# Two chained transformer blocks on one core: products, norms and transposes at a stage's edge taken by groups of 128 tokens, without unread products, with eight slots for split weights

## The reference, cut to what matters

```python
for layer in range(2):                       # first block
    x = x + mixers(rmsnorm(x, norm_mix[layer]) @ w_in[layer])
    x = x + memory_cross_attention(rmsnorm(x, norm_xattn[layer]), ...)
    gate, up = jnp.split(rmsnorm(x, norm_ffn[layer]) @ w_gate_up[layer], 2, axis=-1)
    x = x + (jax.nn.silu(gate) * up) @ w_down[layer]
x = rmsnorm(x, norm_final)
for layer in range(2):                       # second block
    h = swiglu(rms_norm(x, g[0]), ffn_w_in[layer, 0], ffn_w_out[layer, 0])
    x = x + 0.5 * rms_norm(h, g[1])
    h = hybrid_mixer(rms_norm(x, g[2]), ...) if layer == 0 else recurrent_mixer(rms_norm(x, g[2]), ...)
    x = x + rms_norm(h, g[3])
    h = swiglu(rms_norm(x, g[4]), ffn_w_in[layer, 1], ffn_w_out[layer, 1])
    x = x + 0.5 * rms_norm(h, g[5])
```

## Time and profile before

| what | value |
|---|---|
| median of 3 runs | 2314.92 us (2310.24 to 2315.61) |
| the profiled execution's own time | 2307.78 us |
| its span | 2306.3 us |
| mean granted TensorE clock | 0.981 |
| PE busy | 2164.6 us, 94% |
| DVE, ACT busy | 1389.6 us (60%), 1122.4 us (49%) |

### The profile page before, as it was taken

One profiled execution on the slowest core, in us unless ns is written; L12 is line 12 of the kernel. 1 busy time (PEld: TensorE's weight loads), 2 busy tenths in 40 slices (PEclk: granted clock), 3 DMA queues, 4 the chain that ended last, 5 costly groups with the idle time before them and its releaser, 6 DMA issues.

```text
span 2306.3 us, 25337 instructions
## 1 busy us (share of the span) xinstructions
PE 2164.6 (94%) x10018; PEld 1758.5 (76%) x10018; DVE 1389.6 (60%) x1929; ACT 1122.4 (49%) x1741; POOL 33.2 (1%) x45
## 2 busy tenths in 40 slices
PE   8998798999999888999999999979999999979998
PEld 6866677888886667788778877657788788767886
DVE  5966665554695765555455547564655555566553
ACT  5545355444544535544354446534544444475442
POOL 0000000000000000000000000100000000000000
PEclk9999999999999999999999999989999999989999
DMA  6652243555554225355545545303455455534553
GB/s 225 202 198 73 92 165 116 190 189 186 182 183 164 76 89 176 116 184 186 196 157 184 196 169 173 126 37 129 172 185 192 178 184 183 192 127 137 183 185 125
DMA packets 52805, 369.27 MB, mean 160 GB/s; under 512 B 6191, under 2 KB 6447, under 8 KB 9040
## 3 DMA queue, kind: packets, MB, share of 16 engines
q1 hardware_dynamic: 48960, 356.54, 43.4%
q10 hardware_dynamic: 3216, 9.53, 1.3%
q0 software_dynamic: 512, 1.57, 0.3%
HBM read 366.31 MB, written 1.31 MB: 159 GB/s over the span
## 4 chain that ended last, share of the span: by engine, by line
PE 85%; DVE 8%; ACT 5%; issue 1%; DMA 0%; POOL 0%; ACTq 0%; DVEq 0%
PE ps L447 25%; PE ps L449 25%; PE ps L448 25%; PE ps L493 2%; PE ps L549 2%; DVE ring_lo L1023 1%; ACT upper_w L1697 1%; PE ps L658 1%; PE ps L477 1%; DVE x L1173 1%; ACT z L1754 1%; DVE S L1094 1%; DVE xn L1161 1%; PE ps L732 0%; DVE PTs L1108 0%
## 5 line engine op out<-in xcount | busy, mean ns | idle before, releaser
L1023 DVE TENSOR_TENSOR ring_lo<-ring,upper_w 128x1024 fp32r<-128x1024 f32 x659 | 803.4, 1227 | 535.5 <-ACT upper_w L1697 529.9
L1697 ACT CAST upper_w<-ring 128x1024 fp32r<-128x1024 f32 x659 | 689.2, 1054 | 581.1 <-PE ps L449 571.4
L447 PE MATMUL ps<-upper_w,nT_hi 128*128 128x512 f32 x1952 | 776.8, 398 | 29.9 <-DVE nT_lo L1643 15.9
L448 PE MATMUL ps<-ring_lo,nT_hi 128*128 128x512 f32 x1952 | 763.4, 391 | 0.0
L449 PE MATMUL ps<-upper_w,nT_lo 128*128 128x512 f32 (+1 forms) x1824 | 713.9, 391 | 0.0
L447 PEld LDWEIGHTS ps<-upper_w,nT_hi 128*128 128x128 f32 x1952 | 370.4, 190 | 109.0 <-issue 22.1
L448 PEld LDWEIGHTS ps<-ring_lo,nT_hi 128*128 128x128 f32 x1952 | 370.7, 190 | 74.1 <-issue 0.5
L449 PEld LDWEIGHTS ps<-upper_w,nT_lo 128*128 128x128 f32 x1824 | 345.6, 189 | 73.5
L449 PE MATMUL ps<-upper_w,tT_lo 128*128 128x512 f32 (+1 forms) x792 | 308.0, 389 | 0.0
L447 PE MATMUL ps<-upper_w,z_hi 128*128 128x512 f32 x624 | 245.5, 393 | 7.5 <-DVE z_hi L1058 4.8
L448 PE MATMUL ps<-ring_lo,z_hi 128*128 128x512 f32 x624 | 244.3, 391 | 0.0
(11 more groups left out here) (298 smaller groups left out, 1433.2 us busy)
## 6 DMA issues: line engine op xcount, KB each, us to landing
ring<-in_w SPq DMA_DIRECT2D x339, 1024.0 KB, 4.8
big<-in_gains ACTq DMA_DIRECT2D x7, 512.0 KB, 3.6
z<-in_mem ACTq DMA_DIRECT2D x2, 1024.0 KB, 5.2
big<-skew POOLq DMA_DIRECT2D x8, 192.0 KB, 6.7
x<-in_x SPq DMA_DIRECT2D x1, 1024.0 KB, 5.2
xn<-in_w ACTq DMA_DIRECT2D x1, 1024.0 KB, 4.7
out<-x ACTq DMA_DIRECT2D x2, 512.0 KB, 3.1
const<-in_const ACTq DMA_DIRECT2D x1, 529.0 KB, 3.7
```

Of the source, the lines that this page charges most:

```text
L447: PE.matmul(out, hi, w_hi, start=start, stop=False)
L448: PE.matmul(out, hi, w_lo, start=False, stop=False)
L1023: V.tensor_tensor(ring_lo[:, q % RING, cols], ring[:, q % RING, cols], upper_w[:, n % AHEAD, :].bitcast(F32), ALU.subtract).then_inc(*lo_c ...
L1697: A.copy(upper_w[:, n % AHEAD, :], ring[:, q % RING, part * HALF:(part + 1) * HALF]).then_inc(*hi_cut.up(h))
```

## The change

Only the order and place of work changes, at the nine edges behind 0.xo, 0.ffn, 1.xo, 1.ffn, ffn_a, hyb, ffn_b, ffn_c and rec, at the start and at the end:

- The last four halves of a stage are gone through twice, first for token group 0, then for group 1 (`last_halves`); group 0's norm runs meanwhile, and its eight transposes stand before the last half of group 1.
- The first four halves of the next stage are also gone through twice (`by_tokens`); group 1's eight transposes stand before group 0's fourth half. The splits `nT_hi` and `nT_lo` are 16 operations of 128 x 128 in place of 8 of 128 x 256. The weighed sums go to parts of `z` in place of `xn`.
- `keep_on` and its 41 products are gone.
- Four more slots for upper parts, in `S` and `PTs`, are used in the segments that `WIDE` names; there ACT and DVE go four halves ahead, and ACT waits for the half eight before.
- `x` is loaded in two transfers. Ahead of `xo` PE waits for all four rests of the attention's output, not for one after the other. In `recurrent` DVE also waits until PE is through with the part of `nT` that it overwrites.

The core of the diff:

```diff
+    def place(self, wide):
+
+        segs = {h: name for name, span in self.span.items() for h in span}
+        self.wide = [segs[h].startswith(wide) for h in self.split]
+        last, self.slot, self.before = [-1] * 8, [], []
+        for n, wide_ in enumerate(self.wide):
+            s = min(range(8 if wide_ else AHEAD), key=lambda i: (last[i], i))
+            self.slot.append(s)
+            self.before.append(last[s])
+            last[s] = n
+        self.borrowed = {}
+        for n, wide_ in enumerate(self.wide):
+            if wide_ and self.slot[n] >= AHEAD and (self.before[n] < 0 or not all(self.wide[self.before[n]:n])):
+                self.borrowed[n] = segs[self.split[n]].split(".up")[0]
+
+    def limit(self, h):
+
+        n = self.halves[h][2]
+        far = n + AHEAD if n + AHEAD < len(self.split) and self.wide[n + AHEAD] else n + AHEAD - 1
+        while far >= len(self.split) or self.split[far] > self.run_end[h]:
+            far -= 1
+        return far
...
+WIDE = ("0.ffn", "1.in0", "1.ffn", "ffn_a", "hyb.x0", "ffn_b", "ffn_c", "rec.", "ffn_d")
...
+    S_w = twin("S_w", at, [P, 2, HALF])
+    PT_w = twin("PT_w", at, [P, 2, HALF])
...
+    weighed = [z[:, 0, 4608:4608 + D], z[:, 0, 3584:3584 + D]]
+
+    def upper(n):
+
+        s = W.slot[n]
+        return upper_w[:, s, :] if s < AHEAD else S_w[:, s - 4, :] if s < 6 else PT_w[:, s - 6, :]
...
+        def by_tokens(seg, lhs, banks, rows, others=None):
+
+            free(*banks)
+            for t in range(TT):
+                for c, h in enumerate(W.span[seg]):
+                    w_hi, w_lo = weights(h)
+                    if t == 0 and c == 3 and others:
+                        others()
+                    for k in range(2):
+                        f, cols = 2 * c + k, slice(k * BLK, (k + 1) * BLK)
+                        PE.wait_ge(*dve_out.at(f"{rows}.lo{t}{f}"))
+                        m = three(ps[:, banks[t], :], lhs[0](f, TOK[t]), lhs[1](f, TOK[t]), w_hi[:, cols], w_lo[:, cols], f == 0, f == KT - 1)
+                    if t == 1:
+                        m.then_inc(*half_used.up(h))
+
+        def last_halves(name, halves, step, then):
+
+            for t in range(TT):
+                for i, h in enumerate(halves):
+                    w_hi, w_lo = weights(h)
+                    if t == 1 and i == 3:
+                        then(0)
+                    m = step(h, t, w_hi, w_lo)
+                    if t == 1:
+                        m.then_inc(*half_used.up(h))
+                if t == 0:
+                    m.then_inc(*psum_full.up(f"{name}.first"))
+
+        def rows_of(name, src, x_at):
+
+            def then(t):
+                for g in range(2):
+                    b = 4 + 2 * t + g
+                    free(b)
+                    for p in x_at(t, g):
+                        PE.wait_ge(*p)
+                    for i in range(4):
+                        m = PE.transpose(ps[:, b, i * P:(i + 1) * P], src[:, t, (4 * g + i) * P:(4 * g + i + 1) * P], ident)
+                    m.then_inc(*psum_full.up(f"{name}.t{t}{g}"))
+                    held(dve_out.at(f"{name}.lo{t}{4 * g + 3}"), b)
+            return then
...
-        def keep_on(n, b):
-
-            free(b)
-            for i in range(n):
-                PE.matmul(ps[:, b, :], ident, const[:, 0:BLK], start=True, stop=True)
...
-            keep_on(idle, bank)
-            n = parts(f"{f}.n", cols_of(x), KT, ready)
+        def ffn(f, rows, then):
 
             def gated(b):
                 part_group(f"{f}.w", cols_of(z), FT, 2 * b, [dve_out.at(f"{f}.z{b}")], (4, 5))
             for b in range(GU):
                 banks = (2 * (b % 2), 2 * (b % 2) + 1)
-                gemm(f"{f}.up{b}", of_parts(nT_parts), banks, n if b == 0 else (), lambda c: gated(b - 1) if b and c == 2 else None)
+                if b == 0:
+                    by_tokens(f"{f}.up0", of_parts(nT_parts), banks, f"{f}.n", lambda: rows(1))
+                else:
+                    gemm(f"{f}.up{b}", of_parts(nT_parts), banks, (), lambda c: gated(b - 1) if c == 2 else None)
                 held(dve_out.at(f"{f}.z{b}"), *banks)
             for t in range(TT):
                 free(DOWN[t], DOWN[t] + 1)
-            for c, h in enumerate(W.span[f"{f}.down"]):
+            span = W.span[f"{f}.down"]
+
+            def step(h, t, w_hi, w_lo):
+                c = h - span[0]
+                for hf in range(2):
+                    cols = slice(hf * BLK, (hf + 1) * BLK)
+                    m = three(ps[:, DOWN[t] + hf, :], wide_hi(c, TOK[t]), wide_lo(c, TOK[t]), w_hi[:, cols], w_lo[:, cols], c == 0, c == FT - 1)
+                return m
+            for c, h in enumerate(span[:-4]):
                 if c == 2:
                     gated(GU - 1)
                 PE.wait_ge(*dve_out.at(f"{f}.w.lo{c}"))
                 w_hi, w_lo = weights(h)
-                for hf in range(2):
-                    for t in range(TT):
-                        cols = slice(hf * BLK, (hf + 1) * BLK)
-                        m = three(ps[:, DOWN[t] + hf, :], wide_hi(c, TOK[t]), wide_lo(c, TOK[t]), w_hi[:, cols], w_lo[:, cols], c == 0, c == FT - 1)
+                for t in range(TT):
+                    m = step(h, t, w_hi, w_lo)
                 m.then_inc(*half_used.up(h))
+            PE.wait_ge(*dve_out.at(f"{f}.w.lo{FT - 1}"))
+            last_halves(f, span[-4:], step, then)
...
-            for b in range(2):
-                gemm(f"{l}.xo{b}", of_parts(four), (2 * b, 2 * b + 1), n)
-                held(dve_out.at(f"{l}.x_xo{b}"), 2 * b, 2 * b + 1)
-
-        def hybrid():
+            for p in n:
+                PE.wait_ge(*p)
+            free(0, 1, 2, 3)
+            span = [W.span[f"{l}.xo{b}"] for b in range(2)]
+
+            def step(h, t, w_hi, w_lo):
+                b = h in span[1]
+                for k in range(2):
+                    f, cols = 2 * (h - span[b][0]) + k, slice(k * BLK, (k + 1) * BLK)
+                    m = three(ps[:, 2 * t + b, :], four[0][:, f, TOK[t]], four[1][:, f, TOK[t]], w_hi[:, cols], w_lo[:, cols], f == 0, f == 3)
+                return m
+            last_halves(f"{l}.xo", [*span[0], *span[1]], step, ffn_rows[l])
+            for t in range(TT):
+                held(dve_out.at(f"{l}.x_xo{t}1"), 2 * t, 2 * t + 1)
...
+        def lo_rows(name, t, gains):
+
+            for c in range(KT):
+                if c % 4 == 0:
+                    V.wait_ge(*act_out.at(f"{name}.hi{t}{c + 3}"))
+                V.scalar_tensor_tensor(nT_lo[:, c, TOK[t]], ps[:, 4 + 2 * t + c // 4, c % 4 * P:(c % 4 + 1) * P], gains[:, c:c + 1], nT_hi[:, c, TOK[t]].bitcast(F32),
+                                       ALU.mult, ALU.subtract).then_inc(*dve_out.up(f"{name}.lo{t}{c}"))
+
+        def boundary(seg, x_rows, name, gains):
+
+            x_rows(0)
+            cut_first(seg, 3)
+            lo_rows(name, 0, gains)
+            cut_first(seg, 4)
+            x_rows(1)
+            lo_rows(name, 1, gains)
+            mean_square(name, TT, D, 8)
+
+        def added_rows(event, first, last, banks):
+
+            def x_rows(t):
+                V.wait_ge(*(half_used.at(last) if t else psum_full.at(first)))
+                for hf in range(2):
+                    cols = slice(hf * BLK, (hf + 1) * BLK)
+                    V.tensor_tensor(x[:, t, cols], x[:, t, cols], ps[:, banks[t] + hf, :], ALU.add).then_inc(*dve_out.up(f"{event}{t}{hf}"))
+            return x_rows
+
+        def post_rows(f, factor, i, banks=DOWN):
+
+            def x_rows(t):
+                V.wait_ge(*gain_loaded.at(i))
+                V.wait_ge(*act_out.at(f"{f}.h{t}"))
+                V.tensor_scalar(st[:, t:t + 1], st[:, t:t + 1], factor ** -2 / D, factor ** -2 * EPS, ALU.mult, ALU.add).then_inc(*dve_out.up(f"{f}.ms{t}"))
+                V.tensor_tensor(weighed[t].rearrange("p (a n) -> p a n", a=2), ps[:, banks[t]:banks[t] + 2, :], gain.rearrange("p (a n) -> p a n", a=2),
+                                ALU.mult).then_inc(*dve_out.up(f"{f}.w{t}"))
+                own()
+                V.wait_ge(*pool_out.at(f"{f}.post{t}"))
+                for hf in range(2):
+                    cols = slice(hf * BLK, (hf + 1) * BLK)
+                    V.scalar_tensor_tensor(x[:, t, cols], weighed[t][:, cols], st[:, t:t + 1], x[:, t, cols], ALU.mult, ALU.add).then_inc(*dve_out.up(f"{f}.x{t}{hf}"))
+            return x_rows
+
+        def final_rows(t):
+            last_layer(t)
+            V.wait_ge(*act_out.at(f"final.h{t}"))
+            V.tensor_scalar(st[:, t:t + 1], st[:, t:t + 1], 1.0 / D, EPS, ALU.mult, ALU.add).then_inc(*dve_out.up(f"final.ms{t}"))
+            V.wait_ge(*gain_loaded.at(0))
+            V.wait_ge(*pool_out.at(f"final.post{t}"))
+            for hf in range(2):
+                cols = slice(hf * BLK, (hf + 1) * BLK)
+                V.scalar_tensor_tensor(x[:, t, cols], x[:, t, cols], st[:, t:t + 1], gain[:, cols], ALU.mult, ALU.mult).then_inc(*dve_out.up(f"final.x{t}{hf}"))
```

(50 more changed lines are left out.)

298 lines of the change are left out of this document (145 added, 153 removed).

## The result

The changed kernel takes 2289.79 us (median of 4 runs, 2286.89 to 2293.48) against 2315.18 for the kernel before: a ratio of 0.9905, with an interval of 0.9887 to 0.9923. Measured once more among the experiments it is 0.9899 (0.9882 to 0.9915). So it is about 1% faster: 22 us by the first ratio, 23 by the second, 25 by the difference of the medians. The forecast was 2289 and 26 us. The profiled execution took 2291.53 us (span 2290.0), a second one of the same kernel has a span of 2283.5.

What follows compares the result with a forecast made beforehand. PE has no gap inside feed-forward stages; edge gaps total 58.8 us. Gains 18.5 + 4.0 + 0.9 - 2.0 + 1.9 + 2.7 = 26.0 take the profiled 2307.78 to 2281.8; plus 0.31%, 2289 us, 8 in 10 for 2275 to 2306.

Steps and rivals of the forecast that it cites:

- xo: Two starts of xo: PE must have all four rests, begins 1.0 us later each; -2.0 us in all.
- ffn_a: Edge from 1.ffn to ffn_a: 10.9 us becomes 6.9, with waits of 0.8, 3.2 and 0.8; 4.0 us won.
- The edge: Second block's five edges: each falls from 7.6 to 3.9 us, with waits of 1.0 and 0.8; 18.5 us won.
- Short operations: Upper parts of 128 x 128 at the edges: taken at 0.27 us on ACT and 0.275 on DVE.
- upper bound: Rival: short operations cost as much as long ones, edges win 1 us in all, 2314 us; chance 0.10.
- latencies don't overlap: Rival: each short operation takes the long one's whole mean, edges lose 23 us, 2333; chance 0.05 for both slower rivals.
- group 1's whole chain is exposed: Rival: PE waits some 6 us, square to rests, second block wins nothing, about 2307 us; chance 0.03.
- ffn_a to hyb: One of the second block's five edges, forecast like the others at 7.6 to 3.9 us; 3.7 us won.
- The ring: Chunk transfers at the edges: needed 8.0 us after issue, landing after 4.8, later chunks with more slack; no effect.
- The slots' 1.9: Recurrent mixer: with eight slots two casts no longer wait 0.87 and 1.04 us for PE; 1.9 us won.
- The late-chunk rival: A chunk over 8.0 us from issue holds up the edge; at 13.4 us, 2338; chance 0.05 for both slower rivals.
- The clock rival: Every edge lets the clock fall, nine times 1.65 us, gain 11, 2304 us; chance 0.12.

Runs made afterwards that it cites:

- c_xo_each: The changed kernel, but PE waits for each of the four rests ahead of xo just before the products that read it; 2282.15 us, 0.9871 of before.
- l_pe_order: c_xo_each plus e_rec_first, f_fifth_first, group 1's x made before the fourth half's rest, and PE waiting for that rest behind group 1's transposes; 2273.82 us, 0.9836.
- m_clock_a: l_pe_order plus three unread products in the wait at ffn_a and two halves split ahead of the squares at the edge to hyb; 2274.50 us, 0.9834.
- f_fifth_first: c_xo_each, but at edges the fifth half's cast stands ahead of ACT's two squares and its subtraction ahead of DVE's mean; 2280.16 us, 0.9865.
- n_two: e_rec_first and f_fifth_first together; 2274.72 us, 0.9839 of the kernel before.
- e_rec_first: c_xo_each, but in the recurrent mixer the first convolution inputs' copies precede ACT's chunk-waiting cast, DVE's convolution one step earlier; 2280.79 us, 0.9867.
- h_slots_only: The kernel before with only the eight slots for upper parts, order of products, norms and transposes unchanged; 2307.74 us, 0.998.
- a_no_unread: The kernel before with its unread products taken out and nothing else changed; 2316.54 us, 1.002.

## Why the prediction was right, and which steps were off

That the total came out this near is in part luck. The mechanism held at the plain edges and from 0.ffn to 1.in. But xo and hyb won 3.5 and 2.5 us less than forecast, start and end 2.4 more, and at ffn_a and in the mixer two misses cancel.

- **The edge** (7.6 to 3.9): right, 3.7 measured at the second block's plain edges, that is all but the one to hyb. Both waits are where they were put and owed to what was named; their sizes, 0.57 and 0.56, were under the 1.0 and 0.8 forecast, while the rest of the edge took 2.6 and not 2.13. The transposes take 0.79 and 1.05 of it (start to the next product's start, 0.2 of the latter waiting for `x`'s second half). Each wait costs 0.16 more than its bracket, which counts from the end of a product of 0.39 us where the next could have started after 0.227. And four times the first of the new products takes 0.09 us longer.
- **Short operations** at 0.27 and 0.275: measured 0.27 on both engines. The two rivals that hung on them (upper bound; latencies don't overlap) fall. So does the one in which group 1's whole chain is exposed: 0.57 us of it are.
- **ffn_a**: 4.0 won, as forecast, but not by the terms of the sum: the waits were 0.37 and 2.5 us in place of 0.8 and 3.2, and the clock fell in both profiles (0.81 for 7 us in the first), which the text had left open. Here the fall cost 0.5 us (80.91 against 80.38 in c_xo_each, with the same wait and the clock at 1.00), in l_pe_order 1.6 (against m_clock_a).
- **xo** (-2.0): mis-sized, -5.5. With the wait for all four rests PE began 1.16 us later (1.0 forecast), and the step had no term for the clock: together with the wait of 0.88 and the transposes ahead of it, 2.01 us let it fall, and 0.85 didn't. c_xo_each won back 5.4.
- **ffn_a to hyb**: treated as the other four edges, although only hyb.x0 is in `WIDE` and hyb.dt's half is split first. Mis-sized by 2.5 us, of which the longer wait is 1.2; the rest is the clock at the narrow products, for which the sum had no term and which differs from execution to execution (f_fifth_first, n_two).
- **The ring: "Nothing"**: this step failed in the recurrent mixer, in two of its terms. For the later chunks it reckoned the slack by PE; but ACT, one half further ahead, asks for the chunk whose place comes free only in the second pass over rec.in0, and the convolution's copies stand behind that cast. And it took 4.8 us for a transfer where this chunk took 9.2 beside the gates' weights (7.9 in the second profile). e_rec_first took PE's wait for the gates away and won 2.0 us. The slots' 1.9, with the 1.7 of the clock beside them, was right: h_slots_only won 3.5 there. The sum had left the 1.7 out, and nearly as much is lost to the late chunk; so 5.7 against 5.6 in the second profile is luck, and the first, with a longer wait and one more fall of the clock, has 2.9.
- **The late-chunk rival**: no at the edges, where the chunks they need landed 4.7 to 5.0 us from issue (ffn_b to ffn_c); in the mixer it came true in kind, at 3.39 us of ACT's time.
- **End** 2.7, measured 3.7: `x` is complete 4.0 us after the last product (4.3 forecast), but the last transfer also ends sooner, 2.7 us after `x` and not 4.0, as only half of the output is left. **Start** 0, measured 1.3: half a chunk of `x` does come earlier.
- **The clock rival** (every edge lets it fall): no, it stayed at 1.00 at the second block's plain edges and fell at ffn_a, at hyb and at both starts of xo. The Trainium skill ("TensorE: Matmul & The Clock Gate", Part 4: PE-mode transpose) says that transposes don't count as work for the gate. a_no_unread fits that, as sixteen in a row ran at 0.50 to their end, but no run puts products in their place, so it isn't a test.

Against the second profile the sum is 3.2 us too high: 2.5 from hyb and 3.5 from xo, less 2.4 from start and end, 0.6 from the plain edges and 0.1 from the mixer, and 0.3 in untouched stages.
